# A SwiGLU feed-forward stage in a one-core encoder kernel: gate and up as seven block products per slice, down in a second phase

## The reference

```python
def swiglu(h, w_gate_up, w_down):
    gate, up = jnp.split(h @ w_gate_up, 2, axis=-1)
    return (jax.nn.silu(gate) * up) @ w_down
...
        xp = xp + rms_norm(mix, norm_mix_post[l])
        xp = xp + rms_norm(swiglu(rms_norm(xp, norm_ffn_pre[l]), w_gate_up[l], w_down[l]), norm_ffn_post[l])
```

## Time and profile before

| | |
|---|---|
| median of 3 runs | 1616.73 us (1616.28 to 1617.32) |
| the profiled execution's own time | 1615.91 us |
| its span (first to last instruction) | 1614.1 us |
| mean granted clock of TensorE | 0.996 of full speed |
| busy share of the span | PE 97%, weight loads 90%, DVE 45%, ACT 35%, POOL 23% |

### The profile page before, as it was taken

The page is one execution under the profiler, slowest core; times in us unless marked ns, Lnnn a source line. Parts: engine busy times, 40 slices in busy tenths (PEclk is TensorE's granted clock), DMA queues, the critical chain, the costliest instruction groups (busy, mean ns, idle before and its releaser), DMA issues.

```text
span 1614.1 us, 25860 instructions
## 1 busy us (share of the span) xinstructions
PE 1566.3 (97%) x9806; PEld 1449.8 (90%) x9806; DVE 722.4 (45%) x1211; ACT 565.8 (35%) x1237; POOL 379.0 (23%) x264
## 2 busy tenths in 40 slices
PE   6999999999999999999999999999999999999996
PEld 5999999899898989986889989898998989999894
DVE  6564473646557377555532231313223132332318
ACT  6354364655647367343331112021111212111123
POOL 2102112020110211530003223241322314132335
PEclk9999999999999999999999999999999999999998
DMA  6112112121211223452221011111111112011124
GB/s 190 51 54 60 56 46 72 54 63 49 67 55 33 67 72 117 152 181 96 92 92 53 29 50 42 49 52 39 52 39 39 59 32 64 27 52 39 45 99 150
DMA packets 128895, 110.10 MB, mean 68 GB/s; under 512 B 14456, under 2 KB 117152, under 8 KB 128832
## 3 DMA queue, kind: packets, MB, share of 16 engines
q1 hardware_dynamic: 121920, 100.58, 20.1%
q10 hardware_dynamic: 6912, 8.65, 1.5%
HBM read 87.41 MB, written 21.80 MB: 68 GB/s over the span
## 4 chain that ended last, share of the span: by engine, by line
PE 88%; DVE 5%; ACT 5%; issue 2%; DMA 1%; SPq 0%; ACTq 0%; DVEq 0%
PE m_ya L1690 21%; PE m_yb L1690 10%; PE m_yb L1712 10%; PE b_gm L1042 9%; PE a_gm L507 5%; PE m_ya L1712 4%; PE b_gm L1096 4%; PE a_gm L548 4%; PE m_ya L1743 3%; PE m_yb L1743 2%; PE b_ob L1167 2%; PE m_ya L1769 2%; PE m_yb L1769 2%; PE b_tb L1082 2%; PE a_ob L614 1%
## 5 line engine op out<-in xcount | busy, mean ns | idle before, releaser
L1491 POOL TENSOR_TENSOR w_lo<-f_raw,w_hi 128x1024 fp32r<-128x1024 f32 x66 | 157.9, 2399 | 497.4 <-ACT w_hi L1547 497.4
L1690 PE MATMUL m_ya<-x_hi,w_hi 128*128 128x352 f32 x704 | 227.3, 323 | 2.7 <-DVE x_lo L1846 1.6
L1690 PE MATMUL m_ya<-x_hi,w_lo 128*128 128x352 f32 x704 | 225.6, 320 | 0.0
L1690 PE MATMUL m_ya<-x_lo,w_hi 128*128 128x352 f32 x704 | 225.5, 320 | 0.0
L1547 ACT ACTIVATE w_hi<-f_raw 128x1024 fp32r<-128x1024 f32 x66 | 68.2, 1050 | 229.4 <-PE m_yb L1677 221.0
L1690 PEld LDWEIGHTS m_ya<-x_hi,w_hi 128*128 128x128 f32 x704 | 132.0, 188 | 4.1 <-DVE x_lo L1846 1.8
L1690 PEld LDWEIGHTS m_ya<-x_hi,w_lo 128*128 128x128 f32 x704 | 132.3, 188 | 0.4
L1690 PEld LDWEIGHTS m_ya<-x_lo,w_hi 128*128 128x128 f32 x704 | 132.0, 187 | 0.0
L1916 DVE TENSOR_TENSOR f_yacc<-m_yb,f_yacc 128x512 f32<-128x512 f32 (+1 forms) x121 | 83.3, 690 | 74.0 <-PE m_yb L1712 73.7
L1690 PE MATMUL m_yb<-x_hi,w_hi 128*128 128x352 f32 x352 | 113.6, 323 | 0.0
L1690 PE MATMUL m_yb<-x_hi,w_lo 128*128 128x352 f32 x352 | 113.0, 321 | 0.0
(11 more groups left out here) (277 smaller groups left out, 3781.6 us busy)
## 6 DMA issues: line engine op xcount, KB each, us to landing
f_raw<-in_w_gate_up_dram SPq DMA_DIRECT2D x44, 512.0 KB, 3.8
w_raw<-in_w_in_dram SPq DMA_DIRECT2D x32, 512.0 KB, 3.8
f_raw<-in_w_down_dram SPq DMA_DIRECT2D x22, 512.0 KB, 3.5
m_gate<-gate_scratch SPq DMA_DIRECT2D x16, 528.0 KB, 4.4
gate_scratch<-a_gst ACTq DMA_DIRECT2D x24, 176.0 KB, 1.9
gate_scratch<-b_gst ACTq DMA_DIRECT2D x24, 176.0 KB, 1.9
xtok<-in_x_prompt_dram SPq DMA_DIRECT2D x8, 512.0 KB, 4.8
o_xr<-in_x_prompt_dram SPq DMA_DIRECT2D x8, 512.0 KB, 4.2
```

The costliest lines, as they stand in the source:

```text
L1491: pool.tensor_tensor(w_lo[:, j % 3, :, :].rearrange("p k n -> p (k n)"), raw[:, j % 2, :], w_hi[:, j % 3, :, :].rearrange("p k n -> p (k n ...
L1690: last = pe.matmul(gm[c][:, 0:CW], w[:, j % 3, k, :], x[:, k, chunk(c)], start=(k == 0 and n == 0), stop=(k == KT - 1 and n == 2))
```

## The change

The whole feed-forward stage is written anew in two phases.

**Phase one, 22 units, one for each slice.** The gate and up of a slice are seen as a product of two by two blocks: the tokens in two halves of 528 (`t1`, `t2`), the channels in two halves of 4 blocks, the weight columns as gate and up. Instead of eight block products there are seven (`NW`), of sums of blocks. The five sums of input blocks (`X_SUMS`) are made and split once, before or during the first unit: for chunk 0 of 264 tokens by POOL, for chunk 1 by DVE, rounded by ACT, the rest by DVE (`xs`, `x_round`, `x_low`). The five sums of weight blocks (`W_SUMS`) are made by POOL for each slice, and seven blocks of 128 by 512 are rounded by ACT and split by POOL (`w_parts`, `w_round`), each into the slot that the unit before has just read. PE makes each product in two chunks of 264 tokens, 4 blocks by 3 matmuls = 12 matmuls a chunk (`product`), and products 3 to 6 are added onto banks that hold an earlier product. ACT and DVE take partial sums out of the banks and put gate and up together (`copy_v`, `v_add`, `gate_2`, `silu_2`, `copy_up`, `gate_1`, `finish`). The activations of a slice, 128 by 1056, go to a DRAM scratch.

**Phase two, 66 steps.** The token tiles are taken in three groups (0, 1, 2), (3, 4, 5), (sample, 6, 7). In each group all 22 rows of `w_down` and all 22 slices of activations of these tiles come back by DMA, are rounded by ACT and split by POOL and DVE, and PE adds 22 steps into six banks, without a sum in SBUF. A group's normalisation runs in the first steps of the next group. The tiles of the output projection now come in the order 7, sample, 6, 5, 4, 0, 1, 2, 3.

The core of the diff:

```diff
+            X_SUMS = (("11", "22", ALU.add), ("21", "22", ALU.add), ("11", "12", ALU.add),
+                      ("11", "21", ALU.subtract), ("22", "12", ALU.subtract))
+            W_SUMS = {0: ("21", "11", ALU.subtract), 1: ("12", "22", ALU.subtract), 2: ("11", "22", ALU.add),
+                      5: ("11", "12", ALU.add), 6: ("21", "22", ALU.add)}
...
             @block.gpsimd
...
+                def w_parts(it, e, ms=range(NW)):
+                    u = unit(it, e)
+                    for m in ms:
+                        if m in W_SUMS:
+                            if m == 0:
+                                pool.wait_ge(raw_loaded[e], it * 32 + 32)
+                            need(pool, g_done, (u - 1) * UNIT + 2 * (m + 1))
+                            a, b, op = W_SUMS[m]
+                            pool.tensor_tensor(w_whole(m), raw_w(e, a), raw_w(e, b), op).then_inc(w_sum, 1)
+                        pool.wait_ge(w_rounded, u * NW + (m + 1))
+                        whole = w_whole(m) if m in W_SUMS else raw_w(e, W_PLAIN[m])
+                        pool.tensor_tensor(w_flat(m, 1), whole, w_flat(m, 0).bitcast(F32), ALU.subtract).then_inc(w_rest, 1)
...
             @block.scalar
...
+                def step(it, e, ahead):
+                    nxt = (it, 1) if e == 0 else (it + 1, 0)
+                    first = isinstance(it, int) and it == 0 and e == 0
+                    if not first:
+                        copy_v(it, e)
+                        if ahead:
+                            for m in range(3):
+                                w_round(*nxt, m)
+                        for c in range(2):
+                            gate_2(it, e, c)
+                        if ahead:
+                            w_round(*nxt, 3)
+                        for c in range(2):
+                            copy_up(it, e, c)
                     else:
+                        for m in range(4):
+                            w_round(*nxt, m)
                     if ahead:
+                        w_round(*nxt, 4)
+                        w_round(*nxt, 5)
+                    for c in range(2):
+                        gate_1(it, e, c)
+                    if ahead:
+                        w_round(*nxt, 6)
...
             @block.tensor
...
+                BANK = (bg, bu, bm, bg, bu, bg, bu)
+
+                def product(it, e, m, c):
...
                     if c == 0:
+                        pe.wait_ge(w_rest, u * NW + (m + 1))
+                    if first and m >= 2:
+                        pe.wait_ge(x_rest, X_AT.index((m - 2, c)) + 1)
+                    if m == 0:
+                        need(pe, a_step, (u - 1) * 10 + 1 + c)
+                    elif m == 1:
+                        need(pe, a_step, (u - 1) * 10 + 5 + c)
+                    elif m == 2:
+                        need(pe, v_added, (u - 1) * 4 + 3 + c)
+                    elif m == 3:
+                        pe.wait_ge(v_copied, u * 2 + (1 + c))
+                    elif m == 4:
+                        pe.wait_ge(v_added, u * 4 + (1 + c))
+                    elif m == 5:
+                        pe.wait_ge(silu_ready, u * 2 + (1 + c))
                     else:
+                        pe.wait_ge(up_copied, u * 2 + (1 + c))
+                    for k in range(4):
+                        for n, (w, x) in enumerate(((0, 0), (1, 0), (0, 1))):
+                            last = pe.matmul(BANK[m][c][:, 0:CH], w_slot(m, w)[:, k, :], left(m, x, k, c),
+                                             start=(m < 3 and k == 0 and n == 0), stop=(k == 3 and n == 2), skip_group_check=(m >= 3))
+                    last.then_inc(g_done, 1)
...
+                def down(q):
+                    g, f = divmod(q, FT)
+                    pe.wait_ge(w_rest, W_BEFORE + q + 1)
+                    pe.wait_ge(a_rest, q + 1)
+                    for n, t in enumerate(GROUPS[g]):
...
                     if t == NT:
 
                         pe.wait_ge(mix_normed, NT - 2)
-                        for j, c in FIRST[:2]:
-                            gate_up(0, j, c)
+                        pe.wait_ge(h_lo, 10)
+                        pe.wait_ge(s_ready, 8)
+                        step(0, 0, (0,))
+                        pe.wait_ge(mix_normed, NT - 1)
+                        pe.wait_ge(h_lo, 2 * (NT - 1))
+                        product(0, 0, 1, 0)
...
             @block.vector
...
+                def finish(it, e):
...
+                    for c in range(2):
+                        dve.wait_ge(g_done, u * UNIT + (11 + c))
+                        dve.wait_ge(v_added, u * 4 + (3 + c))
+                        dve.tensor_tensor(af(e, 1, c), row(V, c), bg[c][:, 0:CH], ALU.subtract).then_inc(a_step, 1)
+                    for c in range(2):
...
+                        dve.tensor_tensor(af(e, 1, c), af(e, 1, c), row(S2, c), ALU.mult).then_inc(a_step, 1)
...
+                    for c in range(2):
+                        dve.wait_ge(sig_ready, u * 4 + (3 + c))
+                        dve.tensor_tensor(af(e, 0, c), af(e, 0, c), row(S1, c), ALU.mult).then_inc(a_step, 1)
```

More of the change, by code:

```diff
@@ new lines, in unit, with row, af, af_row @@
+            def unit(it, e):
+                return it * 2 + e
+            def row(r, c):
+                return temps[:, r, t1(c)]
+            V, UP, S1, S2 = range(4)
+            def af(e, half, c):
+                return x_whole[1][:, 2 * e + half, t2(c)]
+            def af_row(e):
+                return x_whole[1][:, 2 * e:2 * e + 2, TH:TOKENS]
+            def need(engine, sem, count):
+                if not isinstance(count, int) or count > 0:
+                    engine.wait_ge(sem, count)
@@ L1391, in loads, with load_unit @@
-                def loads(it, ahead):
-                    for j in range(2, NU + 2 if ahead else NU):
-                        sp.wait_ge(lo_done, past(it * NU + (j - 1)))
-                        sp.sem_inc(passed, 1)
-                        load(it + j // NU, j % NU)
+                def load_unit(it, e):
+                    for part in range(2):
+                        src = WGU[:, :, bass.ds(it * (2 * P) + (e * P + part * D_FF), P)]
+                        sp.dma_start(raw_unit(e)[:, part, :].rearrange("p (k n) -> p k n", n=P), src).then_inc(raw_loaded[e], 16)
@@ new lines, in _ @@
+                xs(3)
+                for c in range(2):
+                    silu_2(0, 0, c)
+                x_low(4, 0)
+                x_low(3, 1)
+                for n in range(2):
+                    dve.wait_ge(x1_stored[n], 16 * len(range(n, NT, 2)))
+                xs(4)
+                x_low(4, 1)
+                finish(0, 0)
+                step(0, 1)
+                with dve.Fori(1, NIT) as it:
+                    for e in range(2):
+                        step(it, e)
+                for q in range(STEPS):
+                    low(q)
+                    g, f = divmod(q, FT)
+                    if g and f == 1:
+                        for p in range(3 * g - 3, 3 * g):
+                            normalise(p)
+                    if g and 2 <= f < 5:
+                        add(3 * g - 5 + f)
```

744 lines of the change are left out of this document (478 added, 266 removed).

## The result

The changed kernel takes 1607.2 us (median of 5, 1603.95 to 1609.31), 0.9943 of the kernel before (95% interval 0.9931 to 0.9954): 9.2 us faster, where 22.7 were predicted. The profiled execution has a span of 1605.2 us and a mean granted clock of 0.983.

The account below looks back on a forecast made before the run. PE bounds the kernel before; after, PE and the weight chain lie close. 897.3 + 20 x 20.5 + 265.1 + 4.4 + 14.4 = 1591.2 us of span, 22.9 less, so 1594 us measured; range 1572 to 1618.

Parts of the forecast that it names:

- PE in phase one: Seven products a unit, 168 matmuls of 264 columns at 0.1205 us: 1.446 us a chunk, 20.24 us a unit (20.04 to 20.33).
- The weight chain: POOL and ACT making a unit's weights in turn: 19.8 us undisturbed, 20.7 with DVE; unit taken as 20.5, bounds 20.0 to 21.3.
- its lock: DVE instructions with two SBUF inputs and POOL instructions reading SBUF exclude each other: about 0.9 us a unit for POOL.
- The first two units: Units 0 and 1, with PE waiting for DVE, then ACT's copies: 73.9 us for 40.5 us of matmuls, bounds 62 to 82.
- The 16.1 us: POOL and ACT's time for unit 1's weights from about 863.4, taken as the chain's turn without `gate_2` and `copy_up`.
- Where the stage starts: PE free for the feed-forward stage at 823.4 us, on the clock of the kernel before.
- Phase two: 1144 matmuls of 512 columns, 265.1 us, in steps of 4.17 us, plus 4.4 us of gaps.
- Three places lie open: Phase two: third `w_down` row behind the last slice's store, 1.5 us; bank waits at groups 1 and 2, 1.8 and 1.1.
- hidden: Beside each 4.17 us step of phase two, ACT's 1.05 + 0.52 us, POOL's 2.40 us and 704 KB of loads cost nothing.
- The end: From the last matmul to the end, with the sample and two tiles left: 14.4 us, against 13.4 before.
- fed too slowly: Rival in phase two: late activations add 0.45 us a step, 30 us in all, giving 1624 us; chance 0.05.
- the likeliest case: The forecast for the whole kernel: PE and chain close together, 30 us lost at the start, 1578 to 1610 us; chance 0.55.

Follow-up runs that it names:

- the run with the longer chain: On the changed kernel, POOL makes the second weight sum of a unit twice, from the third unit on: 1.0022 of the kernel before.
- the run with the other start order: On the changed kernel, ACT rounds the seventh weight block and unit 1's first three between roundings of input sums in the first unit: 0.9919 of the kernel before.
- the projection run: On the changed kernel, ACT rounds the first unit's six weight blocks behind a tile's own steps in the output projection: 0.9941 of the kernel before.
- the run with the activations first: On the changed kernel, ACT rounds the activations before the weights in each step of phase two: 0.9915 of the kernel before.
- the edits to phase two, the start and the projection: On the changed kernel, phase two's edits of loads, activations and stores, the first unit's rounding order and the projection's together: 0.9828 of the kernel before.

## Why the prediction was wrong

**PE in phase one: right, a little low.** 1.458 us a chunk where 1.446 was taken between the rows of 256 and 352 columns. A unit takes 20.41 us, without a wait of PE from unit 2 to the last; the forecast had 20.24 for PE alone, at most 20.33.

**The weight chain: right in its place, its lock over-priced.** The forecast put the turn at 19.8 us undisturbed and 20.7 with DVE beside it. It is POOL's two instructions near `finish` that grow, by 0.23 and 0.10 us, 0.33 in a unit and not 0.9; the wait falls on DVE, which has time. So PE binds, with 0.9 us to spare by the run with the longer chain: a turn of 19.5 us. That 20 units came within 1.7 us of the forecast is in part luck, since the 20.5 us were the chain's and the 20.41 are PE's.

**The first two units: right, by their parts too.** 73.7 us against 73.9; unit 0 took 42.6 where 42.2 were predicted, and product 5 of unit 1 started 66.3 us after the first matmul (892.67) where 67.1 were predicted. The 16.1 us that the prediction takes for unit 1's weights are not what it says of them (the turn of 19.8 us without four steps of 0.42 is 18.1); from the first of these roundings to `copy_v` behind the last it was 17.0 (864.80 to 881.82). The granted clock was 0.50 from 836 to 846, from 860 to 866.7, from 880.5 to 887 and from 894.1 to 897.4, where the prediction had 1 us for it: much of that fell into waits, but the last four chunks took 7.4 us in place of 5.8. And the run with the other start order limits what is right here: it moved the roundings by which the prediction's sum sets unit 1, and gained half of what that sum gives. By that run's rows POOL and DVE, which take longer beside each other, take back the rest.

**Where the stage starts: wrong by 3.0 us.** The forecast took 823.4 from the clock of before, so that the projection ahead of it would not change. But the change puts six roundings of weights on ACT into the tiles' chain, 2.5 us by the projection run, and the fall of the clock near 751, to 0.83 over 10 us, cost 1.6 more. Against that the new projection is 0.8 us shorter without either, and it started 0.4 us earlier. The code of the change holds these roundings; the prediction did not price them. The fall could not be read from the trace before, which does not have it.

**Phase two: the step that failed, by 13.2 us.** "Three places lie open", at 1.5 + 1.8 + 1.1 us. The two bank waits came as said: 2.4 us against 2.9. The first place was the right one with the wrong mechanism: not the third row, 1.5 us, but the first two roundings, which stand on ACT behind the last unit's sigmoids, 5.0 us and 1.9 more at the lower level. (The lock does not set this gap: in the run with the activations first it was 4.9 us, for POOL's rest of the weights.) The third row was late as well (3.17 us when the gap was gone), but behind that gap it did not show. And the sentence that calls the step "hidden" counted ACT's 1.57 us and POOL's 2.40 us and left out DVE's rest, and with it the lock that the same prediction had priced in phase one: a mean of 2.40 us over 44 steps in place of 0.55 for 384 columns. In an even run that costs nothing: between the stalls the matmuls start 0.231 us apart. Behind a group's normalisation, beside stores, it made 5.2 us of stalls and 1.6 us of lower clock in the third group. All three of these stalls end with DVE's rest of the sample's 32 columns (L2222), a second one in each step, which only this group has; one rest for both pieces was not tried. The rival "fed too slowly" looked for it in every step, and it sits in three places.

**The end: right.** 14.1 us against 14.4.

The forecast's range for the likeliest case, 1578 to 1610, holds the time, but the gain was under half of what was said. With the edits to phase two, the start and the projection it is 28 us, more than was predicted.

## What to carry to other kernels

Where one stage hands over to the next, look at what stands ahead of the new stage's first instructions on each engine: 5 us lay behind two sigmoids that nothing needed yet. After each such gap is closed, look at the load queue, since the next wait is likely there; an edit that moves nothing alone can be worth 7 us with its partner. Where POOL and DVE split two operands that one engine rounds in a row, let the short one go first (4.5 us here), and price the lock in every stage, not only in the one that looks tight.

## What the runs showed of the hardware

The lock is one-sided in its cost: the later instruction waits out the whole of the earlier one (0.43 to 2.39 us on DVE), while the earlier one keeps its length (POOL's 1024 columns took 2.40 us before and a mean of 2.47 after). It goes the other way too: the two POOL instructions of 2.29 and 3.62 us in the first unit, on 512 columns that take 1.29 us elsewhere, each ended 1.1 us after the DVE instructions beside them. The gap of 5.0 us on PE was followed by nine matmuls at the lower level, mostly 0.43 us apart; after the wait of 2.44 us nine more, from 1545.92 on. In the projection the granted clock fell near 751 in the changed kernel and in seven of the twelve kernels with edits, and stayed at 1.00 in the other five, after a wait of 1.28 to 1.30 us in all thirteen; the kernel before shows no such fall, after 0.80 us. The fall cost 1.6 us in either form of the projection. What decides it was not tried and stays open.
